# Two-layer hybrid decoder step: the first head's queries inside tile 1's output projection, the far output weights on ACT's queue, far merge and late routes shifted by a few groups

## What is computed

```
h = RMSNorm(x); a, b, c = three token mixers of h; g = sigmoid(gate logits of h)
x = x + (g0 * (a @ Wa) + g1 * (b @ Wb) + g2 * (c @ Wc)) @ w_out
q = RMSNorm(x) @ w_query            # 8 heads, 2 halves of 128
s1, i1 = top16(q[:, h, 0] @ keys0.T); s2, i2 = top16(q[:, h, 1] @ keys1.T)
best, expert = top16 of all 16 x 16 sums s1 + s2; gate = softmax(best)
x = x + sum over 8 heads x 16 experts of gelu(h . up[expert]) * gate * down[expert]
```

## Time and profile before

| | |
|---|---|
| median of 3 runs | 5013.13 us (5011.02 to 5021.54) |
| the profiled execution | 5014.03 us, its span 5011.9 us |
| PE busy | 3879.7 us (77%), mean granted clock 0.883 |
| DVE / ACT / POOL busy | 3053.2 / 1165.6 / 1582.5 us |
| DMA | 1539.76 MB, mean 307 GB/s over the span |
| first gather of the first / second layer | 1001.07 / 3428.31 us |
| last gather issued | 4977.4 us |

### The profile page before, as it was taken

How to read it: one execution, slowest core, us unless ns; L and a number is a source line. 1 busy time by engine, 2 the same in 40 slices (tenths; PEclk the granted TensorE clock), 3 DMA queues, 4 the chain that set the end, 5 groups by cost and what they waited for, 6 DMA issues and landing times. The chain is left out here.

```text
span 5011.9 us, 59446 instructions
## 1 busy us (share of the span) xinstructions
PE 3879.7 (77%) x21640; PEld 2183.6 (44%) x21640; DVE 3053.2 (61%) x7365; ACT 1165.6 (23%) x3111; POOL 1582.5 (32%) x1418
## 2 busy tenths in 40 slices
PE   8899999988768555589998897799866865655555
PEld 6766677744224111134475776675432421111111
DVE  6523323277688898754446644435777889985555
ACT  2211221122223222221121222122222322222111
POOL 0412000033333444443340332102333444444443
PEclk9999999999879777799998999999987977777787
DMA  2223232699999999999993234467999999999998
GB/s 111 85 74 116 78 123 81 248 403 408 382 376 406 418 417 419 413 419 419 412 414 156 85 103 169 170 244 302 414 374 380 416 406 412 419 419 418 420 413 349
DMA packets 300422, 1539.76 MB, mean 307 GB/s; under 512 B 29537, under 2 KB 99425, under 8 KB 147617
## 3 DMA queue, kind: packets, MB, share of 16 engines
q0 software_dynamic: 176608, 1263.35, 61.9%
q1 hardware_dynamic: 106784, 257.61, 13.9%
q10 hardware_dynamic: 16736, 14.98, 0.9%
HBM read 1486.85 MB, written 63.20 MB: 309 GB/s over the span
## 5 line engine op out<-in xcount | busy, mean ns | idle before, releaser
L3021 POOL DMA_INDIRECT early<-in_peer,ids x1008 | 1150.0, 1141 | 1917.2 <-PE ps L3219 1352.0
L3219 PE MATMUL ps<-early,diag 64*64 64x512 f32 x7264 | 1139.1, 757 | 699.3 <-ACT diag L3141 699.0
L3056 DVE SCALAR_TENSOR_TENSOR early<-early,rows 128x1024 f32<-128x1024 f32 x1008 | 1219.8, 1223 | 612.5 <-DMA early<-in_peer,ids 610.5
L3219 PEld LDWEIGHTS ps<-early,diag 64*64 64x64 f32 x7264 | 280.2, 158 | 1461.9 <-ACT diag L3141 1033.9
L3141 ACT ACTIVATE diag<-consts_sb,weight 128x64 f32<-128x64 f32 x1152 | 338.0, 340 | 736.5 <-DVE weight L3070 727.6
L1343 PE MATMUL ps<-hT,gate_ring 128*128 128x288 f32 (+2 forms) x1728 | 470.3, 427 | 6.6 <-ACT gate_out L1355 3.4
L3133 ACT ACTIVATE gel<-dot 128x2 f32<-128x2 f32 x576 | 117.2, 204 | 1465.6 <-DVE early L3056 1274.1
L1343 PEld LDWEIGHTS ps<-hT,gate_ring 128*128 128x128 f32 x1728 | 319.5, 195 | 155.1 <-issue 42.6
L3219 PE MATMUL ps<-late,diag 64*64 64x512 f32 x928 | 156.3, 803 | 118.8 <-ACT diag L3141 118.8
L3021 POOL DMA_INDIRECT late<-in_peer,ids x144 | 167.2, 1161 | 208.1 <-PE ps L3219 153.5
L3056 DVE SCALAR_TENSOR_TENSOR late<-late,rows 128x1024 f32<-128x1024 f32 x144 | 174.3, 1223 | 90.5 <-DMA late<-in_peer,ids 90.5
(11 more groups left out here) (423 smaller groups left out, 5774.5 us busy)
## 6 DMA issues: line engine op xcount, KB each, us to landing
gate_ring<-in_in_gate POOLq DMA_DIRECT2D x48, 512.0 KB, 4.4
slot<-in_w_branch SPq DMA_DIRECT2D x16, 1152.0 KB, 7.1
single<-in_peer_query SPq DMA_DIRECT2D x36, 512.0 KB, 8.3
ring<-in_in_delta SPq DMA_DIRECT2D x8, 2048.0 KB, 8.8
early<-in_peer,ids POOLq DMA_INDIRECT x1008, 14.7
slot<-gate_rows SPq DMA_DIRECT2D x16, 864.0 KB, 9.5
slot<-in_in_pool SPq DMA_DIRECT2D x6, 2048.0 KB, 10.6
rest_slot<-in_w_branch SPq DMA_DIRECT2D x16, 768.0 KB, 8.9
```

Source lines behind the costliest of these rows:

```text
L3021: pool.indirect_dma_start(place(q), None, table_rows, bass.IndirectOffsetOnAxis(ap=ids[:, n, c:c + 1], axis=0)).then_inc(s.pair[PLACE[q]], 16)
L3056: nc.vector.scalar_tensor_tensor(out=up, in0=up, scalar=1.0, in1=rows[:, n, :], op0=ALU.mult, op1=ALU.mult, accum_out=dot[:, i % 2, k:k + ...
L3219: last = nc.tensor.matmul(g.ps[k * NS:(k + 1) * NS, 2 * r + m, :], diag[half, q % DIAGS, :], place(q)[half, D + m * 512:D + (m + 1) * 512] ...
```

## The change

The first two queries and scores of tile 0 move, on PE and ACT, to right behind tile 0's transposition, ahead of the second half of tile 1's output projection. On DVE `first_route` moves ahead of the addition of that second half. POOL's wait for both norms moves from gather 0 to gather 5. The far output weights' loads move from SP's list to ACT's, from i = 33 to i = 35. Far merge units 2 to 23 each begin two groups later (2 to 33 in place of 0 to 31); the far output projection stays at 44, 47, 50, 53, 56. The late routes (tile 1's heads 4 to 7 and all of tiles 2 to 4) begin at group 69 in place of 64, with the same spacing.

```diff
     def tensor(self, pe, first_queries, first_scores):
...
                 last.then_inc(s.out_sum, 1)
                 if n and i == 0:
                     self.turn(pe, 0)
+                    first_queries()
+                    first_scores()
...
     def scalar(self, act, first_queries, first_scores):
...
         for n in self.ORDER:
             if n:
                 self.turned(act, nc.scalar.copy, 0, 0)
+                first_queries()
+                first_scores()
...
             for i in range(2):
                 part = g.x[:, n, i * 512:(i + 1) * 512]
+                if n and i:
+                    first_route()
                 dve.wait_ge(s.out_sum, 2 * n + i + 1)
...
-        first_route()
...
-REST_AT = {3 * (m - REST_FIRST) // 2: m for m in range(REST_FIRST, len(REST_UNITS))}
+REST_AT = {2 + 3 * (m - REST_FIRST) // 2: m for m in range(REST_FIRST, len(REST_UNITS))}
...
-OUT_AT = {LOAD_OUT_AT + 11 + 3 * v: v for v in range(len(OUT_UNITS))}
+OUT_AT = {LOAD_OUT_AT + 9 + 3 * v: v for v in range(len(OUT_UNITS))}
...
-    def load_out(self, sp):
+    def load_out(self, act):
...
-        sp.dma_start(self.w_left[:], self.w_o[:, :, 0:512]).then_inc(s.rest_out_in, 16)
-        sp.dma_start(self.w_right[:], self.w_o[:, 0:6, 512:D]).then_inc(s.rest_out_in, 16)
-        sp.dma_start(self.w_last[:], self.w_o[:, 6:KT, 512:D]).then_inc(s.rest_out_in, 16)
+        act.dma_start(self.w_left[:], self.w_o[:, :, 0:512]).then_inc(s.rest_out_in, 16)
+        act.dma_start(self.w_right[:], self.w_o[:, 0:6, 512:D]).then_inc(s.rest_out_in, 16)
+        act.dma_start(self.w_last[:], self.w_o[:, 6:KT, 512:D]).then_inc(s.rest_out_in, 16)
...
     def scalar(self, act, i):
 
         nc, g, s = self.nc, self.g, self.g.s
+        if i == LOAD_OUT_AT:
+            self.load_out(act)
...
-SECOND_EARLY = 4
+SECOND_EARLY, LATE_ROUTES = 4, PH * STEP + 5
...
-    ROUTE_AT.update({PH * STEP + 22 * _i // 5 + k: _head + (k,) for k in range(4)})
+    ROUTE_AT.update({LATE_ROUTES + 22 * _i // 5 + k: _head + (k,) for k in range(4)})
...
                     if q == 0:
                         pool.wait_ge(s.out_sum, 2 * len(out.ORDER))
+                    if q == 5:
                         pool.wait_ge(s.normed, len(out.ORDER))
```

More of the change, by code:

```diff
@@ L2281, in turn, with tensor @@
         last.then_inc(s.turned, 1)
-    def tensor(self, pe):
+    def tensor(self, pe, first_queries, first_scores):
         nc, g, s, merge, merged, w_out = self.nc, self.g, self.g.s, self.merge, self.merged, self.w_out
@@ L2312, in turned, with scalar @@
              g.ps[:, 2 * n + half, :].rearrange("p (k c) -> p k c", k=4)).then_inc((s.hT_a, s.hT_b)[half], 1)
-    def scalar(self, act):
+    def scalar(self, act, first_queries, first_scores):
         nc, g, s = self.nc, self.g, self.g.s
@@ L2433, in load @@
         sp.dma_start(self.gate(m), self.merge.logits[3 * j + b][:, NEAR:TOK]).then_inc(sem, 16)
-    def load_out(self, sp):
+    def load_out(self, act):
         s = self.g.s
-        sp.wait_ge(s.branch_sum, MERGE_UNITS + len(REST_UNITS))
-        sp.wait_ge(s.branch_read, MERGE_UNITS + len(REST_UNITS))
-        sp.dma_start(self.w_left[:], self.w_o[:, :, 0:512]).then_inc(s.rest_out_in, 16)
-        sp.dma_start(self.w_right[:], self.w_o[:, 0:6, 512:D]).then_inc(s.rest_out_in, 16)
-        sp.dma_start(self.w_last[:], self.w_o[:, 6:KT, 512:D]).then_inc(s.rest_out_in, 16)
+        act.wait_ge(s.branch_sum, MERGE_UNITS + len(REST_UNITS))
+        act.wait_ge(s.branch_read, MERGE_UNITS + len(REST_UNITS))
+        act.dma_start(self.w_left[:], self.w_o[:, :, 0:512]).then_inc(s.rest_out_in, 16)
+        act.dma_start(self.w_right[:], self.w_o[:, 0:6, 512:D]).then_inc(s.rest_out_in, 16)
+        act.dma_start(self.w_last[:], self.w_o[:, 6:KT, 512:D]).then_inc(s.rest_out_in, 16)
     def load_gamma(self, sp):
@@ L2980, in _ @@
                     rest.load(sp, LOAD_AT[i])
-                if i == LOAD_OUT_AT:
-                    rest.load_out(sp)
                 if i == GAMMA_AT:
@@ L3118, in ask @@
                     scores(u, a)
-            out.scalar(act)
-            first_queries()
-            first_scores()
+            out.scalar(act, first_queries, first_scores)
             out.turned(act, nc.scalar.copy, 1, 0)
@@ L3232, in sample_sums @@
                 return last
-            out.tensor(pe)
-            first_queries()
-            first_scores()
+            out.tensor(pe, first_queries, first_scores)
             out.turn(pe, 1)
```

## The result

The changed kernel is **slower: 5027.55 us median against 5010.35 for the kernel before, ratio 1.0031 (95% interval 1.0023 to 1.004)**, some 15.5 us by the ratio (the medians differ by 17.2). The forecast was 5009; the median lies just inside the upper end of the range (5028) and in the case "slower", which had 0.20. The intervals of the experiments leave out one execution, of run 12, that took 6856 us.

What follows compares the result with a forecast made beforehand. The DMAs, with a 416 GB/s ceiling, were taken as the bound: time is lost only where their rate falls. From the profiled 5014.0 us, head +18, weights -14 and late routes -9 gave -5: 5009 us, range 4992 to 5028.

Steps and rivals of the forecast that it cites:

- the case "slower": Whole kernel: slower than before, made up of Rival (c) and Rival (d), chance 0.20.
- The bound and the ledger: Expert stages: DMAs bound at 416 GB/s; a stretch L at rate r loses L x (1 - r/416).
- The head, +18: Each layer's start: first gather 5.8 us earlier, but later returns of places and slower PE clock; +18 us both layers (11 to 21).
- The clock's share: PE in the head: idling halves its clock; turn and first query about 3 us slower, group 0's sums 1.7.
- The far output weights, -14: Weights' loads on ACT's queue let `single` have SP's queue alone; -14 us both layers (-20 to 0).
- The 3 us per layer that were to remain: Gap in POOL's issues at the weights: 3 us still lost per layer in place of 8.8 and 11.2.
- The late routes, -9: Behind group 64's fold: taking routes out of groups 64 to 68 saves 4.5 us per layer, -9 both (-3 to -14).
- The far merge's own shift of two groups costs nothing: it fills the same room: Far merge units two groups later: no cost, 0 us; the first far projection stays at 44.
- Rival (c): At the weights, ACT's hold stalls the whole loop, 0 won; head +21, routes -6: +15, 5029 us; chance 0.14.
- Rival (d): Weights on another queue change no transfer, `single` stays late, that part worth 0: +18 - 9, 5023 us; chance 0.06.

Runs made afterwards that it cites:

- run 12: Kernel before with weights on ScalarE's queue, late routes, and the whole far chain (merge units, weights' issue, output projection) two groups later: ratio 1.0003.
- run 6: Kernel before with far output weights issued from ScalarE's queue at group 33 and late routes five groups later, merge and head unchanged: 0.9966, 4992.14 us.
- run 11: Kernel before with weights on ScalarE's queue, issued at group 35 instead of 33, and late routes; merge units and output projection unmoved: ratio 0.9965.
- run 14: Kernel before with weights on ScalarE's queue, late routes, and SP issuing a merge load ahead of the same group's query load: ratio 0.9967.
- run 18: Kernel before with weights on ScalarE's queue at group 33 and late routes, repeated beside the changed kernel: 0.9968, 4995.62 us.
- H: The head's part alone on the kernel before: first queries, tile 0's route and first gathers ahead of tile 1's norm: ratio 1.0031.
- the changed kernel again: The full changed kernel timed and profiled a second time, against the kernel before: ratio 1.0036, profiled at 5029.66 us.
- Run 1: Kernel before with H alone; weights, merge and late routes as before: ratio 1.0031.
- M: The merge's part: far merge units two groups later, the far output projection's groups as before; alone on the kernel before: ratio 0.9992.
- run 9: Changed kernel without M: head's part, weights on ScalarE's queue at group 33, late routes; against the kernel before: ratio 0.9998.
- run 3: Kernel before with only the far output weights issued from ScalarE's queue at group 33 instead of SP's: ratio 0.9976.
- run 2: Kernel before with only the late routes five groups later: ratio 0.9994.
- W: The weights' part: far output weights issued from ScalarE's queue instead of SP's; alone on the kernel before: ratio 0.9976.
- run 5: Kernel before with W and M, weights issued at group 35; head and late routes as before: ratio 1.0009.
- run 4: Changed kernel with the head as before (W, M and late routes), against the kernel before: ratio 0.9998.
- run 13: Changed kernel with SP issuing a merge load ahead of the next query's load on the same group; against the kernel before: ratio 1.0018.
- run 8: Kernel before with far output weights in eight 512 KB issues on ScalarE's queue, one per group from group 33: ratio 0.9981.

## Why the prediction was wrong, step by step

- **The bound and the ledger: right.** Over the 18 runs the dry sum against before's 102.0 gives the measured difference within 6 us in all but one (run 12: -7 by the sum, +1.5 measured); the first profile of the changed kernel is 8 off as well. The four largest gains measured (runs 6, 11, 14 and 18, -16 to -17.5) are the four largest by the sum (-19.5 to -20.4), and the two largest losses are the same too: H +15.0 (+15.5 measured), the changed kernel again +12.7 (+18).
- **The head, +18: right, with its mechanism.** Run 1 measured +15.5 (interval +10 to +20.5). First gather +15.7 (expected +15.7), tile 1's rows +19.1 (+19.2), last query's end +39.5 (37.5 and the clock), gather 6 17.1 us behind gather 5, first return +49.8 (+46.1): six places in flight and then a wait. The clock's share was in it too: turn and first query 2.5 us slower (3 expected; 1.97 and 3.60 against 1.04 and 2.02), group 0's sums 1.7 (1.7 expected). The last of these needs M; in run 9 it isn't there.
- **The far output weights, -14: right for the part alone, -12 in run 3 (interval -6.5 to -17.5), and by the mechanism given: the waits for `single` are gone.** ScalarE was held 16.1 and 17.0 us (17 to 21 expected) and POOL's issues paused 16.34. The 3 us per layer that were to remain were looked for in the gap; about half of what remains lies behind the first far product, at 353 GB/s in run 3. In the changed kernel only -5.5 to -7 are left in that column: M's last unit (group 33) adds its dry stretch there.
- **The late routes, -9: mis-sized.** -3 (interval -7.5 to +1.5) in run 2, -6 in the column, -5 between runs 3 and 6. The fold's own stretch stays at 289 GB/s where it was 284; only what follows it was won. The prediction had 1 us of the gap and 3.5 behind it, per layer; the whole column gives 2.8.
- **"The far merge's own shift of two groups costs nothing: it fills the same room": this is the step that failed.** It measured +16 to +17 in the company of W (run 5 against 3, run 4 against 6, the changed kernel against run 9). The room is not the same: groups repeat with a period of eight in their queries and routes, the merge's units with one and a half, so two groups more put other units beside other queries. Unit 17's load moved from group 19 to 21, behind a wait on SP for a query: that is 4 to 8 us of the 16, by the merge column of run 13. Units 14 and 23 came to stand next to a query on TensorE, and the DMAs run dry there as well; whether that is the rest stays open, for two such pairs in the kernel before cost nothing. The step gave no reason beyond "the same room": it looked neither at what stands beside each unit in its new group nor at the loads that each issues on SP.

With +15.5, -12, -5 and 0 the sum would have been -1.5; with M's +16 it is +14.5, and +15.5 was measured. Rival (c) named the right side and nearly the right time, 5029, but by luck: its mechanism was ScalarE's hold, for which run 8 finds no cost. Rival (d), that the queue doesn't matter, fell with run 3, which is 12 us faster. In the kernel before, the `single` that stands behind the weights on SP's queue was issued only after SP's hold of 21.5 us, and then took 38.1 us to land (37.6 in the first layer), where the median of all `single` loads is 8.3; with the weights on another queue no wait for it is left. The Trainium skill (DMA: Bandwidth & Descriptors, "Issuing engines are not separate DMA queues") says that issuing from several engines saves only the sequencer's time. This trace does not agree: besides the sequencer's time it was the order on the queue that counted.

## What to carry to other kernels

When a step moves by a few places in a woven schedule, list every instruction it issues on every queue, and check for each what stands before it in its new place: here a shift that adds no work cost some 16 us, 4 to 8 of them because a load came to stand behind another load's wait. Price it in the company of the other parts as well: alone it showed no loss, since it also shortened a dry stretch that another part removed anyway. And an earlier first transfer was worth nothing here, since the places that it filled came back later; ask when the first place returns.

## What the runs showed of the hardware that was not expected

A DMA issue held ScalarE for 17.15 us at no cost that could be measured: the same weights in eight issues of 0.38 us, with no hold at all, gave 0.9981 against 0.9976. While ScalarE is held the DMAs go on at 390 to 408 GB/s (whole holds of runs 3 and 6 and of the changed kernel), for the 4 MB of weights are themselves the work. A window of run 6, but for its last 0.8 us inside the hold:

```profile
1226.90:1236.90 10.00, 0.00 (x0) 0.00 (x0) 0.50 (x2) 0.50 (x3) 0.00 (x0) 0.50 1.02 415
```

In these 10 us TensorE does nothing, and its granted clock is 0.50, yet the DMAs move 415 GB/s. The executions of one kernel also spread, by 5 to 31 us from run to run, so that one pair of profiles differed by 4 us where the medians differed by 17; a second profile of the changed kernel (5029.66 us) lay on the other side of its median.
